# Squares summed by matmuls in the opening, and a new order at the handover to attention, in an encoder step on eight cores

## The reference, cut to what matters

```
h = modulate(rmsnorm(x, g_ffn1), sh1, sc1)              # h*(1+scale)+shift
x = x + 0.5 * gt1 * swiglu(h, w_ffn1_in, w_ffn1_out)    # 1024 -> 2 x 2816 -> 1024
h = modulate(rmsnorm(x, g_mix), sh2, sc2)
z = h @ w_in                                            # q, k, v, f, B, C, x, ga, gc
logf = log_sigmoid(z[f] + b_f)                          # forget gate, 16 heads
F = cumsum([past_logf, logf])
s = q k' / 8 + F_q - F_k ; o_attn = softmax(causal(s)) v
m = sigmoid(ga) * o_attn + sigmoid(gc) * (B * short_conv(C * x))
x = x + gt2 * (m @ w_out)
h = modulate(rmsnorm(x, g_ffn2), sh3, sc3)
x = x + 0.5 * gt3 * swiglu(h, w_ffn2_in, w_ffn2_out)
y = rmsnorm(x, g_final)
```

## Time and profile before

| | us |
|---|---|
| median of 3 runs | 1883.65 (1883.44 to 2082.79) |
| profiled execution, its time | 1886.12 |
| its span, slowest core (7) | 1884.6 |
| span of the fastest core (2) | 1872.8 |
| PE busy | 1794.6 (95%) |
| DVE busy, ACT busy | 764.1, 768.6 (41% each) |
| POOL busy | 262.2 (14%) |

### The profile page before, as it was taken

How to read it: one execution, slowest core, us unless ns; L and a number is a source line. 1 busy time by engine, 2 the same in 40 slices (tenths; PEclk the granted TensorE clock), 3 DMA queues, 4 the chain that set the end, 5 groups by cost and what they waited for, 6 DMA issues and landing times.

```text
span 1884.6 us, 35785 instructions; the slowest of 8 cores (1872.8 to 1884.6 us)
## 1 busy us (share of the span) xinstructions
PE 1794.6 (95%) x13248; PEld 957.0 (51%) x13248; DVE 764.1 (41%) x1405; ACT 768.6 (41%) x1492; POOL 262.2 (14%) x337
## 2 busy tenths in 40 slices
PE   3798999999999999999999999999999999999997
PEld 1334545555454565656565656665444444544443
DVE  1333223222268455555555555544652223322255
ACT  2554100111267666666665666665661110011132
POOL 1232100111146300000000000001520000000041
PEclk9988999999999999999999999999999999999998
DMA  9700800897136331313242322233232210422113
GB/s 180 195 4 2 152 12 2 141 162 125 26 146 151 64 83 36 83 36 83 37 94 47 83 51 67 65 120 71 88 57 44 35 29 1 79 34 34 18 59 132
DMA packets 42386, 137.94 MB, mean 73 GB/s; under 512 B 5570, under 2 KB 7972, under 8 KB 39116
## 3 DMA queue, kind: packets, MB, share of 16 engines
q0 software_dynamic: 25456, 81.03, 25.2%
q1 hardware_dynamic: 16760, 54.62, 8.0%
HBM read 180.18 MB, written 36.22 MB: 115 GB/s over the span
## 4 chain that ended last, share of the span: by engine, by line
PE 84%; DMA 4%; DVE 4%; ACT 3%; issue 2%; POOL 2%; DVEq 0%; ACTq 0%; POOLq 0%; SPq 0%
PE pb L464 80%; PE pb L462 4%; DMA RG<-w_ada 2%; DVE tw L667 2%; DMA RX<-xT 1%; ACT H L474 1%; POOL scr L642 1%; ACT scr L474 1%; ACT tw L474 1%; DMA wsall<-w1i 1%; ACT L474 1%; PE pb L1319 0%; ACT RG L474 0%; DVE RX L679 0%; DVE RG L704 0%
## 5 line engine op out<-in xcount | busy, mean ns | idle before, releaser
L464 PE MATMUL pb<-H,wsall 128*128 128x512 bf16 (+1 forms) x5760 | 1159.1, 350 | 26.7 <-ACT H L474 10.8
L464 PEld LDWEIGHTS pb<-H,wsall 128*128 128x128 bf16 x5760 | 513.5, 99 | 525.5 <-issue 51.7
L474 ACT ACTIVATE tw<-pb 128x512 bf16<-128x512 f32 (+3 forms) x320 | 169.3, 532 | 645.7 <-PE pb L464 640.2
L474 ACT ACTIVATE RG<-pb 128x512 bf16<-128x512 f32 (+3 forms) x688 | 345.2, 532 | 174.1 <-PE pb L464 147.3
L464 PE MATMUL pb<-RG,wsall 128*128 128x512 bf16 (+1 forms) x2080 | 388.5, 349 | 0.3
L704 DVE TENSOR_TENSOR RG<-pb,tw 128x512 bf16<-128x512 f32 (+1 forms) x218 | 132.9, 611 | 501.6 <-PE pb L464 444.3
L464 PEld LDWEIGHTS pb<-RG,wsall 128*128 128x128 bf16 x2080 | 186.9, 98 | 199.1 <-issue 5.5
L464 PE MATMUL pb<-RX 68*128 68x512 bf16 (+3 forms) x640 | 214.7, 348 | 1.9 <-ACT RX L474 1.9
L462 PEld LDWEIGHTS pb<-RX,RG 128*128 128x128 bf16 x2176 | 139.0, 97 | 107.1 <-issue 5.8
L718 DVE SCALAR_TENSOR_TENSOR RX<-pb,DER,RX 128x512 f32<-128x512 f32 (+1 forms) x192 | 112.2, 594 | 171.0 <-PE pb L464 167.0
L462 PE MATMUL pb<-RX,RG 128*128 128x65 bf16 x2176 | 169.5, 193 | 2.6 <-ACT RG L474 2.3
(11 more groups left out here) (106 smaller groups left out, 770.0 us busy)
## 6 DMA issues: line engine op xcount, KB each, us to landing
wsall<-w_in POOLq DMA_DIRECT2D x32, 512.0 KB, 5.6
wsall<-w_ada POOLq DMA_DIRECT2D x28, 512.0 KB, 11.2
wsall<-w1i POOLq DMA_DIRECT2D x22, 512.0 KB, 12.5
wsall<-w2i POOLq DMA_DIRECT2D x22, 512.0 KB, 7.6
RX<-xT SPq DMA_DIRECT2D x4, 2048.0 KB
xs<-RX SPq DMA_DIRECT2D x4, 2048.0 KB
kT<-RX SPq DMA_DIRECT2D x32, 256.0 KB
vo<-RX SPq DMA_DIRECT2D x32, 256.0 KB
```

What stands on the lines that cost most here:

```text
L464: ins = e.matmul(o, lhsT=l, rhs=r, start=st, stop=sp)
L474: return P.op("scalar", lambda e: e.activation(out=out, in_=in_, func=func, **kw), reads=reads, writes=writes)
```

## The change

In the opening, for the blocks behind block 1, the squares are made by n_sq (all on ACT, bf16) and summed by eight matmuls, at step 1 and not step 2; the n_mods are at steps 3, 4, 5 and not 4, 5, 6; the cached sums are at step 0 and not 3. n_sum stays in use in the later phases, and the hand-over of its buffers moves there. In the handover the values of block 2 and the queries of block 0 stand in front of f_block(3), the queries of block 1 in front of f_block(4), those of block 2 behind it.

```diff
@@ out_phase
             if norm is not None:
+                alias_seed(B_sqf, B_sq)
                 alias_seed(B_sqs, B_tw[3:5])
@@ opening
         PRE = [[[], [], many("sq", 0, 8), [], many("mod", 0, 2), many("mod", 2, 5), many("mod", 5, 8), []],
-               [many("sq", 0, 4), many("sq", 4, 8), [], [], many("mod", 0, 3), many("mod", 3, 6), many("mod", 6, 8), []]]
+               [many("sq", 0, 4), many("sq", 4, 8), [], many("mod", 0, 3), many("mod", 3, 6), many("mod", 6, 8), [], []]]
         def ahead(tb, j):
             for what, k in PRE[tb > 0][j]:
-                if what == "sq" and tb > 0:
-                    n_sum(tb + 1, k)
-                elif what == "sq":
-                    n_sq(tb + 1, k, k % 2 == 1)
+                if what == "sq":
+                    n_sq(tb + 1, k, tb == 0 and k % 2 == 1)
                 else:
                     n_mod(tb + 1, k, 0, 0)
         for tb in range(5):
-            if tb == 1:
-                alias_seed(B_sqf, B_sq)
             for j in range(JB1):
...
-                if tb < 4 and j == 2:
+                if tb < 4 and j == (2, 1)[tb > 0]:
                     n_stats(tb + 1)
...
-                if tb > 0 and j == 3:
+                if tb > 0 and j == 0:
                     sums[tb - 1]()
@@ handover
         run_mods(wrap(k_units(0, 2)), 8)
         alias_seed(B_ta + B_stx, xcol(3) + xcol(4))
+        run_mods(wrap(v_units(0, 2)) + wrap(q_units(0, 0, True)))
         f_block(3)
-        run_mods(wrap(v_units(0, 2)))
+        run_mods(wrap(q_units(0, 1, True)))
         f_block(4)
-        for tb in (0, 1, 2):
-            run_mods(wrap(q_units(0, tb, True)))
+        run_mods(wrap(q_units(0, 2, True)))
         run_mods(wrap(k_units(0, 3)) + wrap(v_units(0, 3)) + wrap(k_units(0, 4)) + wrap(v_units(0, 4, last=True)))
```

## The result

| | before | after |
|---|---|---|
| median of the runs, us | 1883.65 | 1869.81 |
| profiled execution, its time | 1886.12 | 1868.12 |
| its span, slowest core | 1884.6 (core 7) | 1866.6 (core 5) |
| its fastest core | 1872.8 | 1864.2 |
| PE busy | 1794.6 (95%) | 1787.0 (96%) |

The ratio is 0.9924 (95% interval 0.9895 to 0.9953). The change saves 14 us of the median; the forecast was 19.0. On the profiled execution's own scale the miss is small: a span of 1866.6 against the 1865.6 forecast. In some executions, whatever the kernel, one die is granted less clock (2092.55 us after, 2082.79 before); the two medians of this table count them, and without them are 1883.55 and 1869.23, while all ratios, means over cores and medians further on leave them out.

A forecast was written before the change was run, and what follows sets the result against it. TensorE (PE) was taken to bound the kernel, so only its idle or slow-clock time could be won. Opening -19.5 and handover +0.5 gave -19.0 us, off the median 1883.65: 1864.65 us, range 1858 to 1875.

The forecast's parts named there:

- POOL's wait: Opening: PE's 3.51 us idle before block 2's sum of squares, waiting for POOL's additions; expected to go.
- the border waits: Opening: PE's waits of 3.11, 4.02 and 3.47 us for ACT's last H at the starts of blocks 2 to 4; to go.
- The wait for L704: Opening, block 1: PE waits for DVE's product, queued behind the cached-sums scan; 1.0 us in all, between 0 and 9.3.
- The landing of lfc: Opening, block 1: arrival of the load for the first cached-sums scan, issued at 89.59 us; taken as 92.
- The 0.8 us for block 4: Opening, block 4: the scan at step 0 delays a product where steps last only 0.89 us; 0.8 us lost.
- 19.5 us: Opening: total gain taken for core 7, between two sums of 19.8 and 18.8, all at full clock.
- The prediction's own row for core 1: Opening: core 1 waited only 0.18 us for POOL, so it gains about 14 us and comes to 1864.5.
- +0.5: Handover: net cost in us of moving values and queries ahead of the forget logits, bounds -1 to +3.
- a clock drop: Handover: a stop of some 6 us before the first prompt logits can cost a clock drop of 1.7 us.
- Late lfc: Opening: first scan's load lands at 94 to 101, PE stops 2 to 9 us; time 1868 to 1876, chance 0.12.
- Handover pays: Handover: POOL's chain shortens, rows land earlier, some 4 of 6 us come through; 1860 us, chance 0.07.
- Denser matmuls granted less clock: Opening: denser matmuls on eight cores get less clock; at a granted 0.66 the kernel takes 1908 us; chance 0.02.

The follow-up runs named there:

- opening only: The kernel before with only the opening's part of the change, the handover left as it was: 1868.07 us, ratio 0.9914.
- handover-only run: The kernel before with only the handover's part of the change, the opening left as it was: 1886.56 us, ratio 1.0021.
- other banks: Projections' PSUM banks dealt 0, 5, 6, 7, 1, 2 instead of 5, 6, 7, 0, 1, 2: whole change 1868.83 us, opening's part alone 1867.43 us.
- values ahead: The opening's part on the kernel before, and in the handover only block 2's values put in front of f_block(3): 1868.93 us, ratio 0.9918.

## Why the prediction was right or wrong

**Opening: the mechanism, point by point.** The new opening was to last 84.5 us from the first step behind block 1's x; core 5 has it from 80.2 to 165.2, 85.0. The eight matmuls take 1.89 us with their tail, the forecast 1.73 us each without it. POOL's wait and the border waits went, and the clock was 1.00 on six cores; on cores 1 and 4 it fell to 0.72 between 92 and 98 us. The wait for L704 was forecast at 1.0 us near 94 and is 1.69 us at 94.2 in core 5, 0.58 in core 6, none in core 7 and 2.20 in core 1. The landing of lfc was put at 92: the scan began at 93.96 in core 5, and between 90.17 and 94.11 over the cores. The 0.8 us for block 4 are 0: from 141.84 on there is no wait.

**The step that failed: which core the gain was taken from, and which time it was taken off.** 19.5 us was the gain of core 7 in one execution, in which x of block 2 came late and POOL's wait with its slow matmuls was at its longest. That core did gain 19.0, in part by luck: its first squares of block 2 began at 81.94 before and at 79.06 after. And this execution was 2.5 us above the median, and I took 19.0 off the median all the same. The prediction's own row for core 1 gave about 14 for a core without that accident. Core 1 hit its 1864.5 by luck too, since x came 2.0 us sooner and a stop of 2.20 us with its slower matmuls wasn't in the sum. 15.2 is what the opening's part measured, in the mean core and in the slowest. From the profiled time, 1886.12 - 19.0 gives 1867.1; the profiled time after is 1868.12. The forecast was low by 5.2 us: this step is 4.3 of them (19.5 against 15.2), of which 2.5 are the execution's distance from the median. The handover is 1.1 to 1.9 more, which with this is somewhat over the 5.2; the rest is within the spread of the runs.

**Handover: a term mis-sized.** +0.5 was forecast, within -1 and +3; it measured +3.0 alone and 1.6 (median) to 2.4 (mean core) on top of the opening. The order of events was right: DVE's last scan, the casts behind it, banks that come free late. From POOL's split the last scan was to end at 18.7 us and ended at 18.1; the first prompt logits were to come at 26.4 and came at 25.7. What failed is the next sentence: that a clock drop "can cost" 1.7 us, and was left out of the value taken. First logits to sample step lasted 7.5 us and not 5.7 in the mean of the eight cores. The prediction looked at who holds the sample step, POOL's load; it should have asked also how fast PE works off what lies between. By its own test (over 2 us sooner or later, counted from the scan of block 0) it was wrong here: 33.16 against 30.76 is 2.4 us (in core 7, which it names, 34.04 against 31.75).

**The rivals.** Late lfc: its mechanism did come, a stop of 2.0 to 2.2 us with a fall of the clock, on cores 1 and 4 (3.5 us in core 1), and of 3.68 us in core 5 of opening only. There lfc was not later than forecast (90.83 and 90.54 in cores 1 and 4); PE was ahead. In the change it fell on cores that were not the slowest, so the time that this rival names was met mostly for other reasons. Handover pays: no, the opposite. Denser matmuls granted less clock: no. From 79 to 165 us six cores have 1.00 and the other two 0.98, and the slow matmuls of those two follow a stop. The Trainium skill (TensorE: Matmul & The Clock Gate, the peak-current note) would have had 13/16 here, once three cores of a die run dense matmuls. Core 5 with 84.13 busy us of 86.00 at clock 1.00, and no core of the eight below 0.987 over its whole span, speak against it for this execution.

**What stays open.** What decides whether the clock falls behind the same 3.04 us stop (core 3 of the handover-only run kept it), 0.8 us between the two kernels with other banks, and what n_stats at step 1 is worth by itself.

## What to carry to other kernels

Take the gain of a part from an ordinary core, or from the mean over cores, and take it off the time of the execution it was read from. Filling a wait with later work moves the wait, unless the engines behind it (here DVE's casts, ACT's evictions and its table load) come earlier too; where the moved waits end in one stop, count the clock behind it. And move a stage earlier only together with what makes its input ready: here two edits worth +0.6 and -6.1 us alone saved 12.6 together, and 15 with the sums moved out of their way.

## What the runs showed of the hardware

- After the same stop of 3.04 us, in the same program and execution (handover only), core 3 was granted 1.00 and core 4 0.73 over the next stretch. Behind stops of 0.30 and 1.64 us two cores of eight kept the clock and six fell (0.81 on core 6). In the opening a stop of 3.11 us left the clock at 1.00 (values ahead, core 7), and one of 2.02 us was followed by 0.72 (the change, core 4). So a fall can't be read off the length of the last stop alone.
- The load of lfc, two DMAs issued at 89.78, released the scan at 93.96, 4.2 us later (3.7 to 4.6 over the eight cores); the small row load in the earlier trace rows took 3.0 us.
- The spread between cores goes with the arrival of the opening's loads in good part: the first squares of block 2 begin between 76.4 and 81.9 us in the kernel before, and the cores whose squares came last (5 and 7) are its slowest. In the profile after they begin between 77.6 and 81.7 us, and the cores stand only 2.4 us apart.
